# Scoring the cached index keys first, and projecting the prompt's index rows beside the selection

## The reference

```
aq, ak, av, iq, ik, iw, bq, bf, bi, bg = split(rmsnorm(x) @ w_in)   # 512 columns each; ik 64, iw 8
qi, ki = rope(iq), rope(ik)                                          # 8 index heads x 64, one index key per row
score[t, s] = sum_h iw[t, h] * relu(qi[t, h] . ki[s])                # scaled
idx = top_k(score, 256)         # prompt: 1024 keys, causal; sample: 8192 cached keys and its own new ones
att = softmax attention of 8 heads over the selected keys, gathered
glr = gated linear recurrence over bq, bf, bi, bg
x = x + concat(att, glr) @ w_out
```

## Time and profile before

| | |
|---|---|
| median of three runs | 3259.2 us |
| profiled execution | 3255.71 us, span of the trace 3253.8 us |
| TensorE (PE) busy | 2948.0 us, 91% of the span |
| VectorE (DVE) busy | 1710.3 us, 53% |
| ScalarE (ACT), GpSimd (POOL) busy | 792.4 us, 475.0 us |
| mean granted clock of TensorE | 0.955 of full speed |

### The profile page before, as it was taken

How to read it: one execution, slowest core, us unless ns; L and a number is a source line. 1 busy time by engine, 2 the same in 40 slices (tenths; PEclk the granted TensorE clock), 3 DMA queues, 4 the chain that set the end, 5 groups by cost and what they waited for, 6 DMA issues and landing times. The chain is left out here.

```text
span 3253.8 us, 41975 instructions
## 1 busy us (share of the span) xinstructions
PE 2948.0 (91%) x17344; PEld 2518.8 (77%) x17344; DVE 1710.3 (53%) x2105; ACT 792.4 (24%) x1126; POOL 475.0 (15%) x482
## 2 busy tenths in 40 slices
PE   6898999899788779999999999891799999999998
PEld 3593444465466658999999999891599999999987
DVE  2059998997566543434433434648633333343453
ACT  2132441152356413111111111420311111111232
POOL 1421335565432121000000000000000000000000
PEclk8898999999899979999999999995899999999999
DMA  2252110376411131111111111101111111111011
GB/s 91 59 157 80 53 65 24 98 222 183 151 49 34 41 118 61 49 39 53 40 52 40 52 40 35 46 21 52 33 51 53 40 41 52 40 52 44 24 51 68
DMA packets 160299, 207.62 MB, mean 64 GB/s; under 512 B 17126, under 2 KB 121230, under 8 KB 160093
## 3 DMA queue, kind: packets, MB, share of 16 engines
q1 hardware_dynamic: 145253, 154.38, 15.0%
q0 software_dynamic: 14848, 50.34, 5.2%
HBM read 182.13 MB, written 22.78 MB: 63 GB/s over the span
## 5 line engine op out<-in xcount | busy, mean ns | idle before, releaser
L1991 PE MATMUL ps<-h_split,w_split 128*128 128x352 f32 x7488 | 1215.0, 323 | 17.3 <-DVE w_split L2461 8.2
L1991 PEld LDWEIGHTS ps<-h_split,w_split 128*128 128x128 f32 x7488 | 1205.6, 189 | 24.1 <-issue 11.9
L1991 PE MATMUL ps<-hidden,w_split 128*128 128x352 f32 x3456 | 566.2, 323 | 0.0
L1991 PEld LDWEIGHTS ps<-hidden,w_split 128*128 128x128 f32 x3456 | 558.0, 188 | 0.0
L434 PE MATMUL ps<-w_chunk,hT 128*128 128x512 f32 (+3 forms) x1008 | 402.2, 553 | 26.9 <-DMA w_chunk<-in_w_in 26.9
L434 PEld LDWEIGHTS ps<-w_chunk,hT 128*128 128x128 f32 (+1 forms) x1008 | 170.1, 183 | 234.6 <-issue 202.9
L2499 DVE TENSOR_TENSOR xT<-xT,ps 128x1056 f32<-128x1056 f32 x176 | 220.6, 1253 | 203.0 <-PE ps L1991 202.7
L2478 DVE TENSOR_TENSOR hT<-hT,ps 128x1056 f32<-128x1056 f32 x44 | 55.0, 1254 | 361.4 <-PE ps L1991 361.4
L2352 ACT CAST w_split<-hT 128x2048 fp32r<-128x2048 f32 (+1 forms) x82 | 145.4, 1773 | 388.2 <-PE ps L1991 388.2
L2461 DVE TENSOR_TENSOR w_split<-hT,w_split 128x2048 fp32r<-128x2048 f32 (+1 forms) x82 | 175.0, 2135 | 80.4 <-ACT w_split L2352 79.3
L2488 DVE TENSOR_TENSOR hT<-hT,ps 128x1056 f32<-128x1056 f32 x44 | 55.2, 1255 | 233.8 <-PE ps L1991 233.8
(11 more groups left out here) (338 smaller groups left out, 3079.8 us busy)
## 6 DMA issues: line engine op xcount, KB each, us to landing
hT<-in_w_up SPq DMA_DIRECT2D x44, 1024.0 KB, 5.2
hT<-in_w_down SPq DMA_DIRECT2D x22, 1024.0 KB, 4.8
w_chunk<-in_w_in SPq DMA_DIRECT2D x6, 2048.0 KB, 8.4
hT<-in_w_ple_gate SPq DMA_DIRECT2D x16, 512.0 KB, 3.8
x_rows<-in_x_prompt SPq DMA_DIRECT2D x8, 512.0 KB, 4.4
w_gate_tile<-in_w_in SPq DMA_DIRECT2D x8, 512.0 KB, 5.6
w_out_raw<-in_w_out SPq DMA_DIRECT2D x8, 512.0 KB, 4.3
x_rows<-in_x_prompt SPq DMA_DIRECT2D x16, 256.0 KB, 2.7
```

The lines of the kernel that those rows point to most:

```text
L1991: m = pe.matmul(out, w[a], x[b][:, g * GC:(g + 1) * GC], start=first and i == 0, stop=last and i == 2)
```

## The change

The stages 1 to 4 become two. `load_normalised` is gone as a stage, and so is `project_rows` for iq and ik. `score_sample` now begins with the samples' 32 rows alone: it loads them, normalises them, loads the iq and ik weights into the room of `qT` and `kT` (`index_weights`), projects, rotates and places the queries without a way through memory, and starts on the cached keys. The eight tiles of the prompt's x are normalised and transposed between the key blocks, from a room in `xT`. Keys are transposed two blocks ahead of their multiplication instead of one. Half of the page lists are issued by GpSimd.

`select_sample` then projects iq and ik for the eight prompt tiles first, with the weights that are still on the chip, and the five other chunks behind them. The score steps begin at job 18, two jobs behind the first chunk that is not rotated. The lists move at job 39, the spans at job 44 (before: both at job 28 of 45). `EARLY_BIT` is 17 and `LATE_BIT` 0: a sign step and 14 bits are searched in `select_sample`, 17 bits ahead of the logits, none late.

```diff
-    jobs = [(c, r) for c in chunks for r in range(NT + 1)]
+    jobs = [(c, r) for c in chunks for r in range(NT if c in ("iq", "ik") else NT + 1)]
+    starts = [jobs.index((c, 0)) for c in chunks] + [len(jobs)]
...
+        plain = starts[[c not in rotated for c in chunks].index(True)]
+        first = plain + LAG - 1
...
     def score_steps(j):
-        return range(2 * j, 2 * j + 2) if scores and 2 * j < len(index.steps) else range(0)
+        at = 2 * (j - first) if scores else 0
+        return range(at, at + 2) if scores and 0 <= at < len(index.steps) else range(0)
...
+    held = dict(zip(("iq", "ik"), k.index_weights))
+    fetched = [i for i, c in enumerate(chunks) if c not in held]
...
             for u in score_steps(j):
+                if u == 0:
+                    pe.wait_ge(copied, unplain)
                 index.tensor(pe, u)
...
-EARLY_BIT = 21
-LATE_BIT = 4
+EARLY_BIT = 17
+LATE_BIT = 0
...
+def index_weights(k):
+
+    flat = [x[:].rearrange("p f n -> p (f n)") for x in (k.qT, k.kT)]
+    return [x[:, 0:KD * n].rearrange("p (d n) -> p d n", d=KD) for x, n in zip(flat, (512, IK_COLS))]
...
     @block.gpsimd
     def _(pool):
...
+        src = io["page_table"].rearrange("b (k i) -> i b k", i=16)
+        for s in range(1, 8, 2):
+            pool.dma_start(pages[s:P:8, :].rearrange("p (b k) -> p b k", b=BD), src,
+                           allow_slow_non_contiguous=True).then_inc(pages_landed, 16)
+        pool.wait_ge(indexed, 1)
+        for j in range(4):
+            gather(j)
+        pool.wait_ge(sample_table, 16)
+        rotate(0)
+        rotate(1)
+        for j in range(4, N):
+            gather(j)
...
     @block.tensor
...
+        turn_x(0)
+        pe.wait_ge(x_copied, 1)
+        project(0, w_iq, 512)
+        project(1, w_ik, IK_COLS)
+        turn(0)
+        turn_x(1)
+        turn(1)
+        turn_x(2)
...
     @block.vector
...
+        scale_x(0)
+        dve.wait_ge(pt_landed, 80)
+        dve.wait_ge(pages_landed, 64)
         dve.tensor_scalar(index[:], pages[:], 8.0, k.part[:, 0:1], ALU.mult, ALU.add).then_inc(indexed, 1)
+        copy_x(0)
...
         for j in range(N):
             b, a = j // 4, j % 4
+            t = LEAD + j // 2
+            if t <= NT:
+                (copy_x if j % 2 else scale_x)(t)
             dve.wait_ge(multiplied, j + 1)
...
-    project_rows(k, ctx, block, chunks, scores=True, moves={3 * (NT + 1) + 1: move_lists})
+    project_rows(k, ctx, block, chunks, scores=True, moves={39: gather_candidates, 44: spread_spans})
...
-        best.search(dve, LATE_BIT - 1, 0)
...
-                    k.stage((load_normalised,), (lower_bound,))
-                    k.stage((project_rows, ["iq", "ik"]))
                     k.found = k.sb(proj, "found", [P, QUARTER + TD])
-                    k.stage((score_sample,))
-                    k.stage((select_sample, ["av", "bi", "bg", "aq", "ak"]))
+                    k.stage((lower_bound,), (score_sample,))
+                    k.stage((select_sample, ["iq", "ik", "av", "bi", "bg", "aq", "ak"]))
```

More of the change, by code:

```diff
@@ L173, in load_constants @@
     k.lb_logit = [k.vec[:, 8 * KD + i * BH:8 * KD + (i + 1) * BH] for i in range(2)]
[L178 to L244, removed]
@@ L372, in project_rows, with weights @@
     stored = k.sem_ring(ctx, "rows_stored", RAW)
-    projected, taken, roped, turned, copied, iw_stored = k.sems(
-        ctx, "projected", "taken", "roped", "turned", "copied", "iw_stored")
+    projected, taken, roped, turned, copied = k.sems(ctx, "projected", "taken", "roped", "turned", "copied")
+    chunk_of = [i for i in range(len(chunks)) for _ in range(starts[i], starts[i + 1])]
+    unplain = sum(starts[0] <= j < plain for j in nth_rot) if scores else 0
+    held = dict(zip(("iq", "ik"), k.index_weights))
+    fetched = [i for i, c in enumerate(chunks) if c not in held]
+    def weights(i):
+        c = chunks[i]
+        return held[c] if c in held else w[:, fetched.index(i) % 2]
     def stores_before(j):
@@ L417, in turn @@
             pe.wait_ge(roped, t + 1)
-            if scores and t == 0:
+            if scores and t == unplain:
                 pe.wait_ge(index.rectified, len(index.steps))
@@ L484, in _ @@
     def _(pool):
-        if scores:
-            for u in range(len(index.steps)):
-                index.pool(pool, u)
         for j, (c, r) in enumerate(jobs):
+            if scores and j == plain:
+                for u in range(len(index.steps)):
+                    index.pool(pool, u)
             if c not in rotated:
@@ L1357, in _ @@
         sp.wait_ge(placed, 16)
+        sp.wait_ge(index_stored, 16)
+        sp.wait_ge(tables, 16)
     @block.gpsimd
@@ L1361, in _, with gather @@
         view = io["cache_kidx"][0].rearrange("g (s e) d -> (g s) (e d)", s=8)
-        pool.wait_ge(indexed, 1)
-        for j in range(N):
+        def gather(j):
             if j >= 4:
@@ L1371, in _, with turn_x @@
     def _(pe):
[L1372 to L1378, removed]
+        def turn_x(t):
+            r = order[t]
+            n = rows_of(r)
+            pe.wait_ge(x_scaled, t + 1)
+            if t:
+                pe.wait_ge(x_copied, t)
+            if t == LEAD:
+                pe.wait_ge(new_summed, 1)
+            for d in range(KD):
+                m = pe.transpose(ps[:, 6 + d // 4, (d % 4) * P:(d % 4) * P + n], rows[0:n, t % 3, d * P:(d + 1) * P], k.ident[0:n, 0:n])
+            m.then_inc(x_turned, 1)
@@ L1380, in turn, with project @@
+        def project(n, w, cols):
+            pe.wait_ge(w_landed[n], 16)
+            for d in range(KD):
+                m = pe.matmul(ps[0:NS, 2 + n, 0:cols], hT[:, d, SEQ:R], w[:, d, :], start=d == 0, stop=d == KD - 1)
+            m.then_inc(projected, 1)
         def turn(j):
```

187 lines of the change are left out of this document (148 added, 39 removed).

## The result

The changed kernel takes 3218.7 us (median of four runs, 3216.77 to 3221.04) against 3259.76 of the kernel before (the median of its three runs and a fourth): a ratio of 0.9875 (95% interval 0.9858 to 0.9892), 41 us less. The forecast was 3212, in a range from 3200 to 3229. The profiled execution took 3216.77 us, its span is 3214.9; the profiled execution before, 3255.71, less the forecast 47.5 gives 3208.2, so 8.6 us are to be found.

What follows compares the result with a forecast made beforehand. Serial pieces up to 625 us, with TensorE waiting between them, were taken as the bound. The next stage's first matmul 47.0 us earlier plus 0.5 in the attention, off 3259.2, gave 3212 us; 8-in-10 range 3200 to 3229.

Steps and rivals of the forecast that it cites:

- TensorE's selection: Selection stage: old chunks 360.9 us, added iq and ik jobs 58.5 and 14.8, small waits; 436.7 us from the stage's start.
- the lists: Selection: candidate lists move at 266 us from the stage's start, landed at 270, then a merge of 27.7 us.
- Start: Chain ahead of the looped key blocks: weights, page lists, projection, rotations, transposes; first looped block at 39.5 us.
- the sum: Start of the program: weights landed at 15.0, four page lists 2.7 behind them, two VectorE instructions 1.0: 18.7 us.
- I add 1.5 us for the places where they collide: Loop of key blocks: allowance for x work on ScalarE and VectorE colliding or late key gathers; loop end 130.5 us.
- VectorE in the selection: Selection: rounds, merge, spans landed by 305, rows and sign, fourteen steps at 6.77 us; VectorE ends at 428 us.
- the 8 us of room: End of the selection: four moved search steps fit ahead of TensorE's 436.7 us, with 8 us to spare.
- VectorE ends the selection: Rival, selection's end: fourteen steps at 7.30 us and a slower merge, up to +10 us, 3215 to 3222; chance 0.07.
- The late start: Rival, program start: page lists hold up the first gathers and shift everything, +7 to +15 us, 3219 to 3227; chance 0.10.
- Attention: Samples' attention: ends on gathered values, not VectorE, so dropping four late steps gives -0.5 us (bounds -4 and +4).
- The removed steps: Rival, samples' attention: VectorE's four late steps had set its end, so 24 us more would go, 3188; chance 0.03.
- The loop did not turn serial: Denies a rival, loop of key blocks: no overlap, 5.6 us a block, loop 179 instead of 85 us, kernel 3306; chance 0.02.

Runs made afterwards that it cites:

- Busy fillers: Changed kernel plus 53 added identity transposes on TensorE, nobody reading them, where it stood idle ahead of the loop of key blocks: 3215.8 us, ratio 0.9869.

## Why the prediction was right, and where it missed

The mechanism was right: the scoring first, the projections beside the selection. The runs bear out VectorE's maximum 100 us earlier, TensorE's selection (436.1 us from the stage's start to the last fold against 436.7), the lists (410.42 - 142.03 = 268.4 against 270), and the attention that doesn't care for the late steps.

*Start.* That the loop began at 39.87, where 39.5 was forecast, was in part luck. The iq weights did not land near 15.0: where TensorE waited for them alone, its projection began at 17.63 to 18.16. SP's four page lists took 7.71 us (7.45 to 15.16), not 2.7. The page numbers were still turned into row numbers at 18.57, near the 18.7 of the sum, because the two errors are not added: the lists landed beside the late weights, not behind them. The projection then took 8.57 us and not 10.09, and from its end to the first block it was 12.1 us and not 10.7.

*Loop.* "I add 1.5 us for the places where they collide" was the wrong cause and too little. Hardly anything collided (TensorE is busy for 82.46 of the 82.72 us behind 50.68): two blocks with a tile of x take 6.35 us (66.22 to 72.57) against 5.2 later in the loop, where no tile is left. But the first 10.81 us ran at a granted clock of 0.55, a loss of 4.9 (0.45 of 10.81), of which the 85.3 us taken over from before held about 1.4 (the 3.48 us at 149.48 against twice 1.04). Busy fillers removed it. I had seen the low clock in the earlier trace rows, and had put it on the projection and on the selection's first job, not on the loop. Behind the loop came 1.2 us more, 1.0 of it at the change of stages (1.82 against 0.87 us idle).

*VectorE in the selection.* 428 was forecast for its end, 439.5 measured: 5.1 by spans that land at 310.1 instead of 305 (they were issued at 301.0, close to the 300.5 forecast, and took 9.1 us to land), and 6.3 by steps 7.22 instead of 6.77 us apart. Thirteen of the fourteen meet GpSimd's rotations: their two last instructions, which turn the counts into the next threshold, take 0.37 to 0.80 and 1.14 to 1.15 us, and those of the last step, behind the last rotation, 0.17 and 0.17. In the run with four more steps, all steps that end behind the last rotation take 0.17 and 0.17 there. So the 8 us of room were not there, and the rival "VectorE ends the selection" came true in part, for 1.9 us instead of up to 10. The rule of the Trainium skill's page "SBUF — State Buffer" (Who interferes with whom), by which I had 436, agrees better with the trace than the average that I took.

*The late start* did not come at its price of 7 to 15 us. The lists held the projection up by 1.4 us, and only because VectorE's copy of the samples' rows stood behind them in its queue.

*Attention.* -2.3 in this pair, -0.5 forecast; profiles of the changed kernel's 17 steps give 213.4 to 215.7, so the 2.3 us are not clear of that scatter. The removed steps were not worth their time, as two experiments show (the old split in the changed kernel, the new one in the kernel before). The loop did not turn serial.

*The unchanged part.* It took 2413.4 us in the profile of before and 2416.6 to 2424.4 in those of the changed kernel and of all experiments but the one with 67 transposes. The kernel before with the new split alone, whose code there is the old one, took 2416.8, and the profiled execution before lay 3.5 us below its median. So the 4.4 us of this pair are no effect of the change that any run here shows. By medians, 41 us were gained of 47.5 forecast.

## What to carry to other kernels

When work is moved to the front of a program, price the start at the clock that its waits bring, not at the clock of the loop it is copied from. Where an engine is to fill another's shadow, look at the smallest transfer that it waits for and at what its queue issues just ahead. A gain of 2 us in one place is seen in the trace and not in the total; take several such together before timing them.

## What the runs showed of the hardware

The number of TensorE's instructions ahead of a place can change the time there. With 67 added transposes ahead of 39 us instead of 53, the waits at four places from 1440 us on rose from 5.4 to 16.0 us, and for three of the four long ones the profile names nothing that ended them. The part behind the attention took 2438.4 us against 2418.4, and all five runs lay between 3228.9 and 3231.4. Only none, 53 and 67 were tried. The Trainium skill's page "Runtime: NRT & Kernel Launch" (Instruction fetch mechanics) says that an engine's instructions are fetched in blocks while it executes and that crossing a block is mostly hidden. No run here shows the fetch at work; if it is that, 4 us at a time were not hidden.

In the changed kernel TensorE stood for 2.19, 1.32 and 1.61 us ahead of 39 us, and the granted clock was 0.50 from 39 to 45 us. In two profiles with the same fillers the longest such piece was 1.92 and 2.04 us; the clock from 39 to 45 us was 0.50 in the first and 0.98 in the second. In the three profiles whose fillers left pieces of 0.78 us at most from 29 to 51 us, it was 1.00 there.
